# Forming the norms' factors as exp(-ln/2) on ScalarE, in place of sqrt on ScalarE and reciprocal on VectorE

## What is computed

```python
def _rmsnorm(x, g):
    x32 = x.astype(jnp.float32)
    y = x32 * lax.rsqrt(jnp.mean(x32 * x32, axis=-1, keepdims=True) + EPS)
    return (y * g.astype(jnp.float32)).astype(x.dtype)
```

## Time and profile before

| | |
|---|---|
| median of 3 runs | 1018.73 us (1015.61 to 1020.45) |
| the profiled execution's own time | 1012.11 us |
| its span, first to last instruction | 1010.3 us |
| PE busy | 933.9 us, 92% of the span |
| DVE busy | 643.7 us, 64% |
| ACT busy | 508.7 us, 50% |
| mean granted TensorE clock | 0.971 of full speed |

### The profile page before, as it was taken

How to read it: one execution, slowest core, us unless ns; L and a number is a source line. 1 busy time by engine, 2 the same in 40 slices (tenths; PEclk the granted TensorE clock), 3 DMA queues, 4 the chain that set the end, 5 groups by cost and what they waited for, 6 DMA issues and landing times.

```text
span 1010.3 us, 18019 instructions
## 1 busy us (share of the span) xinstructions
PE 933.9 (92%) x7517; PEld 883.8 (87%) x7517; DVE 643.7 (64%) x999; ACT 508.7 (50%) x729; POOL 2.9 (0%) x6
## 2 busy tenths in 40 slices
PE   5599899899999999988999999998988789999997
PEld 2487687799999998865899999998988789999997
DVE  0655474686767677774875665566966776655664
ACT  3525963565555568574543434354645554343432
POOL 1000000000000000000000000000000000000000
PEclk9799999999999999897999999998999899999999
DMA  9977566475555569311376556554441446555531
GB/s 351 329 222 245 169 242 235 148 242 181 190 188 189 187 183 176 90 45 42 125 232 208 169 173 207 185 167 137 139 142 58 149 128 209 173 205 206 169 126 42
DMA packets 134637, 176.90 MB, mean 175 GB/s; under 512 B 19792, under 2 KB 116348, under 8 KB 134428
## 3 DMA queue, kind: packets, MB, share of 16 engines
q1 hardware_dynamic: 133932, 173.97, 52.6%
q10 hardware_dynamic: 624, 1.77, 0.6%
HBM read 174.68 MB, written 1.05 MB: 174 GB/s over the span
## 4 chain that ended last, share of the span: by engine, by line
PE 76%; DVE 10%; ACT 6%; DMA 5%; issue 3%; SPq 0%; DVEq 0%; ACTq 0%
PE psum L1476 23%; PE psum L1477 22%; PE psum L1478 22%; DVE w_lo L876 3%; DMA raw<-in_w_in_dram 2%; DMA raw<-in_w_ada_dram 2%; PE psum L1563 1%; ACT w_hi L503 1%; PE psum L1768 1%; PE psum L1579 1%; PE psum L1779 1%; PE psum L1820 1%; DVE h_lo L908 1%; ACT h_hi L514 1%; DVE work L917 1%
## 5 line engine op out<-in xcount | busy, mean ns | idle before, releaser
L1476 PE MATMUL psum<-h_hi,w_hi 128*128 128x256 f32 x1384 | 397.4, 287 | 35.9 <-DVE h_lo L1030 10.3
L1477 PE MATMUL psum<-h_lo,w_hi 128*128 128x256 f32 x1384 | 392.7, 284 | 0.0
L1478 PE MATMUL psum<-h_hi,w_lo 128*128 128x256 f32 x1384 | 392.0, 283 | 0.0
L503 ACT ACTIVATE w_hi<-raw 128x2048 fp32r<-128x2048 f32 (+1 forms) x139 | 264.4, 1903 | 151.3 <-PE psum L1478 104.0
L876 DVE TENSOR_TENSOR w_lo<-raw,w_hi 128x2048 fp32r<-128x2048 f32 (+1 forms) x139 | 313.1, 2276 | 3.5 <-ACT w_hi L503 3.4
L1476 PEld LDWEIGHTS psum<-h_hi,w_hi 128*128 128x128 f32 x1384 | 266.7, 193 | 45.7 <-issue 34.4
L1477 PEld LDWEIGHTS psum<-h_lo,w_hi 128*128 128x128 f32 x1384 | 267.0, 193 | 0.2
L1478 PEld LDWEIGHTS psum<-h_hi,w_lo 128*128 128x128 f32 x1384 | 266.7, 193 | 0.0
L1476 PE MATMUL psum<-a_hi,w_hi 128*128 128x256 f32 x688 | 192.3, 279 | 0.4 <-DVE w_lo L876 0.4
L1477 PE MATMUL psum<-a_lo,w_hi 128*128 128x256 f32 x688 | 192.0, 279 | 0.0
L1478 PE MATMUL psum<-a_hi,w_lo 128*128 128x256 f32 x688 | 192.0, 279 | 0.0
(11 more groups left out here) (272 smaller groups left out, 826.5 us busy)
## 6 DMA issues: line engine op xcount, KB each, us to landing
raw<-in_mlp_w_in_dram SPq DMA_DIRECT2D x32, 1024.0 KB, 5.4
raw<-in_mlp_w_out_dram SPq DMA_DIRECT2D x32, 1024.0 KB, 6.7
raw<-in_w_ada_dram SPq DMA_DIRECT2D x24, 1024.0 KB, 7.1
raw<-in_w_up_dram SPq DMA_DIRECT2D x22, 1024.0 KB, 5.2
raw<-in_gla_w_in_dram SPq DMA_DIRECT2D x12, 1024.0 KB, 5.8
raw<-in_w_down_dram SPq DMA_DIRECT2D x11, 1024.0 KB, 5.5
raw<-in_w_in_dram SPq DMA_DIRECT2D x10, 1024.0 KB, 8.1
raw<-in_w_out_dram SPq DMA_DIRECT2D x4, 1024.0 KB, 5.4
```

The costliest lines, as they stand in the source:

```text
L503: act.activation(halved(w_hi, m % SPLIT_SLOTS, SPLITS[m]), halved(raw, r % RAW_SLOTS, SPLITS[m]), ACT.Copy).then_inc(*mark("w_hi", m))
L1476: pe.matmul(dst, lhs[0], rhs[0], start=start, stop=False, skip_group_check=True)
L1477: pe.matmul(dst, lhs[0], rhs[1], start=False, stop=False, skip_group_check=True)
L1478: return pe.matmul(dst, lhs[1], rhs[0], start=False, stop=stop, skip_group_check=True)
```

## The change

At every place where the factor was a square root followed by a reciprocal, ACT now takes `Ln` of the same input with the same scale and bias, waits for it, and takes `Exp` with scale -0.5 of the result; DVE's reciprocals are gone, and DVE waits for ACT's exponential instead. The requests for the set `sqrt_and_others` are gone or replaced by `natural_log_exp_and_others`, and with them the request in `gate(0)`. `v_norm`, `head_root` and `finish` contain no request of their own. Cut to its core:

```diff
@@ ACT
             def total(i):
                 act.wait_ge(*at("job", "sum", i))
-                dst = rstd
-                act.activation(dst[:, :], bank("sum", i)[:, 0:S], ACT.Sqrt, scale=1.0 / D, bias=cst("eps"))\
+                act.activation(rstd[:, :], bank("sum", i)[:, 0:S], ACT.Ln, scale=1.0 / D, bias=cst("eps"))\
                     .then_inc(*mark("act_read", "sum", i))
+                act.wait_ge(*at("act_read", "sum", i))
+                act.activation(rstd[:, :], rstd[:, :], ACT.Exp, scale=-0.5).then_inc(*mark("rstd", i))
...
-                act.preload_act_table_set("sqrt_and_others")
+                act.preload_act_table_set("natural_log_exp_and_others")
...
-                copy(("sum", i), rstd[:, :], ACT.Sqrt, scale=1.0 / D, bias=cst("eps"))
+                total(i)
...
             def v_norm():
                 act.wait_ge(*at("v_sum", 0))
-                act.activation(small[:, 8:16], small[:, 0:8], ACT.Sqrt, scale=1.0 / HD, bias=cst("eps"))\
-                    .then_inc(*mark("v_root", 0))
+                act.activation(small[:, 8:16], small[:, 0:8], ACT.Ln, scale=1.0 / HD, bias=cst("eps"))\
+                    .then_inc(*mark("v_log", 0))
+                act.wait_ge(*at("v_log", 0))
+                act.activation(small[:, 8:16], small[:, 8:16], ACT.Exp, scale=-0.5).then_inc(*mark("v_rstd", 0))
...
             def project(kind, n):
                 ahead((kind, n))
-                if n == 0:
-                    act.preload_act_table_set("sqrt_and_others")
+                if kind == "gla_out" and n == 0:
+                    act.preload_act_table_set("natural_log_exp_and_others")
 
             def add_down(*key):
-                act.preload_act_table_set("natural_log_exp_and_others" if key[0] == "down" else "sqrt_and_others")
+                if key[0] == "down":
+                    act.preload_act_table_set("natural_log_exp_and_others")
...
                 act.wait_ge(*at("gate_abs", h, 1))
-                if h == 0:
-                    act.preload_act_table_set("natural_log_exp_and_others")
...
             def head_root(h):
                 act.wait_ge(*at("job", "gla_sum", h))
-                act.activation(work[:, h, :], bank("gla_sum", h)[:, 0:S], ACT.Sqrt, scale=1.0 / S, bias=cst("eps"))\
+                act.activation(work[:, h, :], bank("gla_sum", h)[:, 0:S], ACT.Ln, scale=1.0 / S, bias=cst("eps"))\
                     .then_inc(*mark("act_read", "gla_sum", h))
+                act.wait_ge(*at("act_read", "gla_sum", h))
+                act.activation(work[:, h, :], work[:, h, :], ACT.Exp, scale=-0.5).then_inc(*mark("gla_rstd", h))
...
@@ DVE
-            def total(i):
-                dve.wait_ge(*at("act_read", "sum", i))
-                dve.reciprocal(rstd[:, :], rstd[:, :]).then_inc(*mark("rstd", i))
...
-            def root(i):
-                dve.wait_ge(*at("act_read", "sum", i))
-                dve.reciprocal(rstd[:, :], rstd[:, :]).then_inc(*mark("rstd", i))
...
             def head_norm(h):
-                dve.wait_ge(*at("act_read", "gla_sum", h))
-                dve.reciprocal(work[:, h, :], work[:, h, :]).then_inc(*mark("gla_rstd", h))
                 dve.wait_ge(*at("gla_rstd", h))
```

More of the change, by code:

```diff
@@ L847, in finish @@
                 act.wait_ge(*at("last_sum", 0))
-                act.activation(small[:, 70:72], small[:, 68:70], ACT.Sqrt, scale=1.0 / D, bias=cst("eps"))\
-                    .then_inc(*mark("last_root", 0))
+                act.activation(small[:, 70:72], small[:, 68:70], ACT.Ln, scale=1.0 / D, bias=cst("eps"))\
+                    .then_inc(*mark("last_log", 0))
+                act.wait_ge(*at("last_log", 0))
+                act.activation(small[:, 72:74], small[:, 70:72], ACT.Exp, scale=-0.5).then_inc(*mark("last_rstd", 0))
             steps = {"setup": setup, "ada": ada_sums, "turn_x": turn_x, "angles": angles, "add_down": add_down, "root": root, "scaled": scaled,
@@ L1064, in v_norm @@
                     .then_inc(*mark("v_sum", 0))
-                dve.wait_ge(*at("v_root", 0))
-                dve.reciprocal(small[:, 8:16], small[:, 8:16]).then_inc(*mark("v_rstd", 0))
                 dve.wait_ge(*at("v_rstd", 0))
@@ L1429, in finish @@
                     .then_inc(*mark("last_sum", 0))
-                dve.wait_ge(*at("last_root", 0))
-                dve.reciprocal(small[:, 72:74], small[:, 70:72]).then_inc(*mark("last_rstd", 0))
                 dve.wait_ge(*at("last_rstd", 0))
@@ L1442, in _ @@
             steps = {"setup": setup, "rows": columns, "angles": angles, "w_sp": mask_w_sp, "in": take_in, "down": down, "qkv": qkv,
-                     "gla": gla, "mlp_up": mlp_up, "mod": modulation, "gains": gains, "root": root, "scaled": scaled, "rope": rope,
+                     "gla": gla, "mlp_up": mlp_up, "mod": modulation, "gains": gains, "scaled": scaled, "rope": rope,
                      "v_norm": v_norm, "gate_mix": gate_mix, "stick_a": stick_a, "stick_b": stick_b,
                      "stick_c": stick_c, "win_a": win_a, "win_b": win_b, "win_d": win_d, "split": split, "split_lo": split,
-                     "unscaled": unscaled, "tree": tree, "sums": sums, "total": total, "r_cols": r_cols,
+                     "unscaled": unscaled, "tree": tree, "sums": sums, "r_cols": r_cols,
                      "project": project, "ff_up": ff_up, "mlp_act": mlp_act, "add_down": add_down, "q_b": q_b,
```

## The result

The kernel before took 1013.06 us in the median of 20 runs (1008.97 to 1020.45), the changed one 1020.45 (1012.32 to 1022.81). The ratio is **1.0055, 95% interval 1.0039 to 1.0071**: slower by 5.6 us, 4.0 to 7.2. The median of before is lower here than the 1018.73 of its first three runs, and the two medians of this table lie 7.4 us apart where the ratio gives 5.6; the kernels are compared by the ratio. The profiled execution of the changed kernel took 1016.60 us, its span is 1014.8.

What follows compares the result with a forecast made beforehand. PE's work plus its short waits was taken to bound the kernel; the terms 0.2 - 1.3 - 0.2 - 0.35 + 2.85 + 0.95 + 1.6 - 0.2 = +3.55 us, added to the 1018.73 median, gave 1022.3 us, range 1016 to 1027.

Steps and rivals of the forecast that it cites:

- `v_norm`, +0.2: At `v_norm`, the new load replaces the one ahead of L646, so only the small exponential adds: +0.2 us, bounds 0 and 1.5.
- `root(1)`, -1.3: At `root(1)`, PE's 3.03 us wait shortens as the factor comes earlier, and the gain lasts: -1.3 us.
- `total(4)` and `total(6)`, -0.2 each: At these two stages, only PE's 0.20 us wait behind the reciprocal goes: -0.2 us each, no more to be had.
- `total(5)` and `gate(0)`, -0.35: At the gates, a 1.28 us load goes, but DVE then waits nearly 1 us for PE at `r_col`: -0.35 us.
- Heads 0 and 1: First `head_root` pair: added loads delay ACT's copy of `mix` 3, hence DVE's reads and PE: +2.85 us, bounds 0 and 3.85.
- Heads 2 and 3: Second `head_root` pair: four loads outweigh the two reciprocals removed: +0.95 us, bounds -3.5 and +2.
- The clock, +1.6: In `gla` 11, PE's wait growing from 1.60 to 4.45 us brings a stretch at lower clock: +1.6 us.
- rival 1: After the longer wait, the low clock lasts through all of `gla` 11 and beyond: +5.7 us, total 1026.4; chance 0.20.
- The four other requested loads, `root(0)` and `finish`, 0: Loads ahead of `out` and `wo` and behind the second block's feed-forwards, plus the `root(0)` and `finish` factors: worth 0.
- Rival 2: Loads between logarithm and exponential at the heads cost nothing, so the kernel gets faster: -6.85 us, 1011.9; chance 0.07.
- Rival 3: Table switches cost more than their load, twice the price on the heads' path: +7.7 us on top, 1030; chance 0.04.
- Rival 4: Clock doesn't fall behind the heads' delay, or `gate(0)` yields its full 1.28 us: sum about 1, 1019.5; chance 0.19.

Runs made afterwards that it cites:

- ninth: The kernel before with only the `v_norm` part of the change put in; 1013.84 us, ratio 0.9993.
- tenth: The changed kernel with `v_norm` put back to square root and reciprocal; 1019.71 us, ratio 1.0051.
- eighth experiment: The kernel before with `total(5)` alone by Ln and Exp, the common set requested ahead of it, the load ahead of `gate(0)` left out; 1013.69 us, ratio 1.0004.
- fourth experiment: The changed kernel with nine unused matmuls of constants in PE's wait before chunk `gla` 11; 1016.15 us, ratio 1.0014.
- first experiment: The changed kernel with the set holding logarithm and exponential requested once ahead of each pair of head norms; 1008.11 us, ratio 0.9937.
- seventh: The changed kernel with the common set requested at heads and `v_norm`, plus eight unused matmuls in PE's wait at the gates; 999.99 us, ratio 0.9862 to the kernel before.

## Why the prediction was right

Forecast were +3.55 us, a ratio of 1.0035 on the median then known; measured 1.0055 (1.0039 to 1.0071), and 1020.45 us lie within 1016 to 1027. That the time comes so near the forecast of 1022.3 is in part luck: the base of three runs was 5.7 us above the median of 20, and the effect was sized too small, by 2 us in the ratio and 3.8 in the medians; these errors partly offset each other. In the ratio, which is free of the base, the direction and the parts are right and the sum is small: 1.0035 lies just below the interval. The likeliest case lay on the near side of the 0.5% line and the measured value lies just beyond it, on the side that had been given 0.29, with an interval that reaches to both sides. DVE's busy time fell by 15.6 us (predicted 15.7). By the traces the stages sum to 0.10 - 1.34 - 0.47 - 0.28 + 6.06 - 0.47 = +3.6, with 6.06 the mean of the heads' stages over the four traces that have the new `head_root` as it is in the change (4.94, 6.30, 6.58, 6.42).

- *`v_norm`, +0.2*: +0.10, and by the ninth and tenth experiments nothing measurable. Right in mechanism: the new load took an old one's place. What the bounds of 0 to 1.5 left out was the other side: three of the four loads there were not needed, and 2.6 us of the wait were to be had, nearly 4 with the clock behind it.
- *`root(1)`, -1.3*: -1.34 in all four of the table's traces that have it. PE's wait is 1.69 in place of 3.03 (1.7 forecast), and the gain holds at the next chunk, as worked out.
- *`total(4)` and `total(6)`, -0.2 each*: -0.47 each. The wait of 0.20 is gone, but the row's idle time isn't the whole price of a wait: in the trace of before two matmuls start 0.48 us apart at it and the next two 0.22, where 0.12 is usual there. These are 0.46 us lost. A term mis-sized by 0.27.
- *`total(5)` and `gate(0)`, -0.35*: -0.28; DVE waits 0.88 us at `r_col` in the changed kernel (0.94 in the eighth experiment), where "nearly 1 us" was predicted. Most of the load's 1.28 us is lost there. PE's wait before `gla` 8 is 3.74 where 3.6 was forecast.
- *Heads 0 and 1, +2.85*: +2.75, and +2.69 or 2.70 in the others. The path was as described: ACT's loads, the copy of `mix` 3 (2.7 us later, 2.9 forecast), DVE's reads, PE (a wait of 4.30, some 4.4 forecast).
- *Heads 2 and 3, +0.95*: +1.0 to 1.1, read in the fourth experiment, where the clock is out of the way. The silus didn't hold the gates up: the six of L1419 run in 2.09 us without a pause.
- *The clock, +1.6*: this term was too small. The changed kernel's own trace has 2.19 for clock and second pair together, so 1.1 to 1.2; the other three have 3.61, 3.88 and 3.72, so 2.5 to 2.8. The mean over the four is 2.3; in the fourth experiment, with PE busy in the first wait, there is nothing of it. Read for `gla` 11 alone, from 773.09 to 793.26, which is what the term was meant for, the four have 2.53, 3.44, 3.62 and 3.51 with the second pair in them, less its 1.0 so 1.5 to 2.6: the forecast 1.6 was one of the cases, at their lower end. What I had not allowed for is that the same two waits cost 1 us more than before in one execution and nearly 3 in the next; rival 1 (+5.7 for `gla` 11) is further off than any of them.
- *The four other requested loads, `root(0)` and `finish`, 0*: right as far as the traces tell. Where these loads stood, the offset of the changed kernel moves by 0.15 us at most (3.65 at 150 and 3.54 at 188, 0.96 at 474 and 0.83 at 504, 0.36 at 512 and 0.37 at 687, 4.45 at 836 and at the end).
- *Rival 2, that the inner loads cost nothing*, was wrong of this kernel, yet the first experiment made it true by hand, and its numbers held: it had PE's wait before `gla_out` shrink to 2.4 us (2.29), the first wait stay at 1.60 (1.60), and 5.0 us gained in the heads (5.2); its sum of -6.85 us is a ratio of 0.9933, and 0.9937 was measured. The Trainium skill, "ScalarE: Activation LUTs", section "Table sets: the hidden batching unit", counts one load for ln and then exp; the trace has one between each logarithm and its exponential until the common set is asked for, and then one for four functions.
- *Rival 3*: the rows show each load 1.28 us long and the next instruction 0.01 us behind it, and each load in the heads starts 0.02 us behind the end of what stands ahead of it, so no extra price. The drain of about 1380 ns that the Trainium skill, "ScalarE: Activation LUTs", section "What ACT_TABLE_LOAD costs", adds to a load isn't seen in these traces.
- *Rival 4, nothing to be seen*: neither of its conditions held in the changed kernel. A lower stretch followed the wait before `gla` 11 in all four traces with that wait, and the gates gave 0.28 and not 1.28. The fourth experiment, with PE kept busy in the wait, is the case it described.

What stays open: the measured ratios of the changed kernel (1.0055), of all but `v_norm` (1.0051) and of all but the heads (0.9995) all lie 1.5 to 2 us above the sums of their stages (1.0036, 1.0035, 0.9977). The first and the last sum lie 0.0003 and 0.0002 below their intervals, the second lies inside. Not every kernel has this rest: in the fourth experiment sum and measurement agree (1.0013, 1.0014), and with one load at `v_norm` more was gained than the stages' sum gives. One part may lie behind `v_norm`: the lower clock followed the wait there in all five traces with the new form and in three of the five with the old one (one of the two exceptions is the profile that all sums go by). One profile for each kernel can't show more, and none of the runs isolates it.

**A version that beats both.** The change with the common set asked for at the heads and ahead of `v_norm`'s stage takes 1001.26 us where before takes 1013.66 (0.9871); with PE kept busy at the gates 999.99 (0.9862), which the runs can't tell from the former.

## What to carry to other kernels

A square root and a reciprocal replaced by a logarithm and an exponential are worth what DVE's 1.75 us less ACT's 0.42 are on PE's path, less the table loads that come with it: count the loads in the order of instructions, and where both functions are to share a set, ask for it by name, ahead of the wait, since the build put a load ahead of every logarithm and every exponential where no common set was asked for. Price the clock along with a wait of PE that grows, with a spread and not a number, because the same waits cost 1 us here and 3 us there. And before a difference of two traces is put down to the change, look at it in a second trace of an unchanged kernel, in stages short enough to leave out the stretches in between.

## What was unexpected of the hardware

- The same wait of PE is followed by the lower clock in one execution and not in the next: 3.23 us before 120.89, then 1.00 over 121 to 127 in the first profile of before, and 0.55 us for the first matmul in the second. In the changed kernel that stretch reads

```profile
121.00:127.00 6.00, 5.91 (x28) 5.40 (x32) 3.56 (x6) 5.69 (x8) 0.00 (x0) 0.50 0.00 0
```

  against 45 matmuls at 1.00 before. The wait of 2.29 us before `gla_out` had full clock behind it in the first experiment, but not in the seventh, where the matmul behind it lasted 0.55 us as well:

```profile
782.54 0.55 PE L1471 MATMUL psum<-h_hi,w_hi 128*128 128x256 f32 x1 [2.29 <-DVE h_lo L911]
```

- Matmuls of constants that nobody reads, in place of idle time, kept the clock at full and gave 1.1 to 2.8 us at the heads (fourth experiment, against the four traces without them) and 1.5 at the gates (seventh), at no price that the traces show in the work around them.
